# Sums of squares added up before TensorE, mLSTM gates on four column groups, and head scalings one step sooner

## The reference, cut to what matters

```python
def rms_norm(x, g):
    y = x * rsqrt(mean(x * x, axis=-1) + NORM_EPS)
    return y * g
...
def forgetting_attention(h, k, v, F, w_qg, q_gain, w_o):
    q = rms_norm(split_heads(q), q_gain)      # k likewise, in shared_kv
    s = einsum('bhqd,bhkd->bhqk', qb, k) * sm_scale + Fq - F
    p = softmax(where(kpos <= qpos, s, -inf))
    return einsum('bhqk,bhkd->bhqd', p, v)
...
def mlstm_inputs(...):
    # r: direction, h: head, e: 512 of the head, g: 8 = 4 input + 4 forget gates
    gates = (einsum('bhne,rheg->rbng', q, wq_g) + einsum('bhne,rheg->rbng', k, wk_g)
             + einsum('bhne,rheg->rbng', v, wv_g))
```

## Time and profile before

| | us |
|---|---|
| median of 3 runs (lowest, highest) | 2857.6 (2853.48, 2858.82) |
| profiled execution, its own time | 2853.31 |
| its span in the trace | 2851.5 |

### The profile page before, as it was taken

One profiled execution on the slowest core, in us unless ns is written; L12 is line 12 of the kernel. 1 busy time (PEld: TensorE's weight loads), 2 busy tenths in 40 slices (PEclk: granted clock), 3 DMA queues, 4 the chain that ended last, 5 costly groups with the idle time before them and its releaser, 6 DMA issues. The chain is left out here.

```text
span 2851.5 us, 36974 instructions
## 1 busy us (share of the span) xinstructions
PE 2675.0 (94%) x15206; PEld 2110.7 (74%) x15206; DVE 1320.5 (46%) x1833; ACT 756.1 (27%) x1408; POOL 1485.0 (52%) x474
## 2 busy tenths in 40 slices
PE   5899778999999999899999899999999999999998
PEld 4777777788887866678888786867676457878787
DVE  7747357665522315438454465415067855121211
ACT  4653321312201124423111123222223433011210
POOL 3653715677776752158777542422264027755574
PEclk9999979999999999999999899999999999999999
DMA  5222226465532221035555122222153226321221
GB/s 232 85 88 61 59 71 273 184 234 223 221 133 74 89 75 44 15 112 229 219 210 191 60 100 82 93 88 86 66 184 114 103 105 242 127 87 60 74 103 60
DMA packets 84048, 353.25 MB, mean 124 GB/s; under 512 B 26680, under 2 KB 38968, under 8 KB 46016
## 3 DMA queue, kind: packets, MB, share of 16 engines
q1 hardware_dynamic: 66048, 242.65, 23.3%
q10 hardware_dynamic: 17856, 108.54, 10.0%
HBM read 316.55 MB, written 34.60 MB: 123 GB/s over the span
## 5 line engine op out<-in xcount | busy, mean ns | idle before, releaser
L488 POOL TENSOR_TENSOR whi<-wraw,con_sb 128x2048 fp32r<-128x2048 f32 x170 | 615.5, 3620 | 1266.4 <-PE ps L544 1061.3
L490 POOL TENSOR_TENSOR wlo<-wraw,whi 128x2048 fp32r<-128x2048 f32 x170 | 802.2, 4719 | 13.3
L544 PE MATMUL ps<-hh,whi 128*128 128x512 f32 x952 | 372.6, 391 | 5.0 <-DVE hl L1760 5.0
L544 PE MATMUL ps<-hl,whi 128*128 128x512 f32 x952 | 370.9, 390 | 0.0
L544 PE MATMUL ps<-hh,wlo 128*128 128x512 f32 x952 | 370.9, 390 | 0.0
L544 PEld LDWEIGHTS ps<-hh,whi 128*128 128x128 f32 x952 | 179.1, 188 | 45.9 <-DVE hl L1760 5.4
L1976 DVE TENSOR_TENSOR midl<-rsq,midh 128x512 fp32r<-128x512 f32 x64 | 154.6, 2420 | 113.6 <-ACT midh L1934 113.6
L544 PEld LDWEIGHTS ps<-hh,wlo 128*128 128x128 f32 x952 | 179.0, 188 | 37.5
L544 PEld LDWEIGHTS ps<-hl,whi 128*128 128x128 f32 x952 | 179.2, 188 | 36.8
L544 PE MATMUL ps<-midh,whi 128*128 128x512 f32 x512 | 200.4, 391 | 0.0
L544 PE MATMUL ps<-midh,wlo 128*128 128x512 f32 x512 | 200.0, 391 | 0.0
(11 more groups left out here) (432 smaller groups left out, 5155.8 us busy)
## 6 DMA issues: line engine op xcount, KB each, us to landing
wraw<-wst SPq DMA_DIRECT2D x174, 1024.0 KB, 4.8
cond_w<-wcond ACTq DMA_DIRECT2D x68, 1024.0 KB, 4.8
first_w<-wcond SPq DMA_DIRECT2D x8, 1024.0 KB, 19.2
mod_w<-wcond SPq DMA_DIRECT2D x8, 1024.0 KB, 13.5
d_v<-ssb ACTq DMA_DIRECT2D x4, 1536.0 KB, 5.1
d_s<-ssb ACTq DMA_DIRECT2D x4, 1536.0 KB, 5.0
sld<-d_s SPq DMA_DIRECT2D x4, 1536.0 KB, 8.3
vld<-d_v SPq DMA_DIRECT2D x16, 384.0 KB, 3.3
```

The source lines that it names most:

```text
L488: pool.tensor_tensor(whi[:, s], wraw[:, f], C("zero").broadcast_to([P, BLK]), ALU.add).then_inc(sem("w_high"), 1)
L490: pool.tensor_tensor(wlo[:, s], wraw[:, f], whi[:, s].bitcast(F32), ALU.subtract).then_inc(w_split, 1)
L544: o = e.matmul(ps[:, b, :nt], w[:, k, mc], x[:, k0 + k, t0:t0 + nt], start=first and k == 0 and j == 0, stop=final and k == nk - 1 and j == 2)
```

## The change

Four edits. (1) The ring of four `sq` buffers becomes a total (`sq[:, 3]`, where square 0 is written) and a ring of three. DVE adds squares 1 to 6 to the total (`add_square`, behind each x tile's update); TensorE sums the total and square 7 alone, 4 matmuls each, both behind the last block. DVE waits for each square. (2) `squares_of_x` issues a one-element Sqrt (`sqrt_table`) ahead of the last Square. (3) The gates: the 16 columns are laid into a 32-column weight tile, the four feature tiles m of a source go to four groups of 32 output partitions, and `region` joins the four groups by a matmul with a 0/1 matrix (`C("gates")`, 64 KB more in the constants) ahead of the bias. (4) The attention: `scale(i+1, 0)` stands ahead of the turns at t = 1, and q and k are both scaled and normed at t = 1.

```diff
-                part = wif[d, t, c].reshape(4, P, 8).transpose(1, 0, 2)
-                gate[0, :, 4 * t:4 * t + 4, 64 * d:64 * d + 4] = part[:, :, :4]
-                gate[0, :, 4 * t:4 * t + 4, 64 * d + 32:64 * d + 36] = part[:, :, 4:]
+                gate[0, :, 4 * t:4 * t + 4, 8 * d:8 * d + 8] = wif[d, t, c].reshape(4, P, 8).transpose(1, 0, 2)
...
+    c["gates"] = np.zeros((P, P))
+    for j in range(4):
+        c["gates"][GW * j + np.arange(16), gate_row[0]] = 1.0
...
+        def sqrt_table(e):
+            e.activation(started[:, 0:1], C("zero"), ACT.Sqrt)
+
+        def squares_of_x(e, squared, added, beside=None):
             for k in range(KT):
+                if k == KT - 1:
+                    sqrt_table(e)
                 e.wait_ge(*AC.need(acc_free[k % NACC]))
+                if k >= 4:
+                    e.wait_ge(*added.at(k - 3))
+                    if beside is not None:
+                        e.wait_ge(*beside.at(k - 2))
+                e.activation(sq_ring[k % 3] if k else sq_total, x_sb[:, k], ACT.Square).then_inc(*squared.inc())
+        def add_square(e, k, squared, added):
+            if not 0 < k < KT - 1:
+                return
+            e.wait_ge(*squared.at(k + 1))
+            if k > 1:
+                e.wait_ge(*added.at(k - 1))
+            e.tensor_tensor(sq_total, sq_total, sq_ring[k % 3], ALU.add).then_inc(*added.inc())
...
             for j in range(4):
                 block(j)
-                for k in (2 * j - 2, 2 * j - 1):
-                    if k >= 0:
-                        square_sum(e, k, squared, summed)
-            square_sum(e, KT - 2, squared, summed)
-            square_sum(e, KT - 1, squared, summed)
+            e.wait_ge(*added.at(KT - 2))
+            sum_of(e, sq_total, 0, True, False)
+            e.wait_ge(*squared.at(KT))
+            sum_of(e, sq_ring[(KT - 1) % 3], 0, False, True).then_inc(*summed.inc())
...
+                    more = t == 1 and i + 1 < KT
+                    if more:
+                        scale(i + 1, 0)
                     turn(2 * s)
                     turn(2 * s + 1)
                     if t == 0 and i:
                         values(i - 1)
                         spread_sums(i - 1)
-                    elif t in (1, 2) and i + 1 < KT:
-                        scale(i + 1, t - 1)
+                    elif more:
+                        scale(i + 1, 1)
...
-                    elif t in (1, 2) and i + 1 < KT:
-                        norm(i + 1, t - 1)
+                    elif t == 1 and i + 1 < KT:
+                        norm(i + 1, 0)
+                        norm(i + 1, 1)
...
-                                o = pe.matmul(ps[:, b, :nt_], wg[:, 4 * j + m], src[:, m, t0:t0 + nt_],
-                                              start=j == 0 and m == 0, stop=j == 2 and m == 3)
+                                o = pe.matmul(ps[GW * m:GW * m + GW, b, :nt_], wg[:, 4 * j + m], src[:, m, t0:t0 + nt_],
+                                              start=j == 0, stop=j == 2)
...
+                for b, (t0, nt_) in zip((6, 7), spans):
+                    pe.matmul(ps[:, b, :nt_], C("gates"), gacc[:, t0:t0 + nt_], start=True, stop=True).then_inc(*gates_summed.inc())
...
-                step(dve.tensor_scalar(gz[:], gacc[:], V("bif", 0), None, ALU.add), sem("gz_ready"))
+                for b, (t0, nt_) in zip((6, 7), spans):
+                    dve.wait_ge(*gates_summed.at(b - 5))
+                    o = dve.tensor_scalar(gz[:, t0:t0 + nt_], ps[:, b, :nt_], V("bif", 0), None, ALU.add)
+                    o.then_inc(*VE.up(sem("gz_ready")))
```

More of the change, by code:

```diff
@@ L1667, in add_to_x, with add_to_x_once @@
             VE.loop(e, n // 4, four)
-        def add_to_x_once(e, gate):
+        def add_to_x_once(e, gate, squared, added):
             for m in range(KT):
@@ L1675, in add_to_x_once, with sum_of, summed_blocks @@
                                        ALU.add).then_inc(*VE.up(acc_free[b]))
-        def squares_of_x(e, squared, summed):
+                add_square(e, m, squared, added)
+        sq_total, sq_ring = sq[:, 3], [sq[:, j] for j in range(3)]
+        def sqrt_table(e):
+            e.activation(started[:, 0:1], C("zero"), ACT.Sqrt)
+        def squares_of_x(e, squared, added, beside=None):
             for k in range(KT):
+                if k == KT - 1:
+                    sqrt_table(e)
                 e.wait_ge(*AC.need(acc_free[k % NACC]))
-                square(e, k, x_sb[:, k], squared, summed)
-        def summed_blocks(e, block, squared, summed):
+                if k >= 4:
[10 more added lines that the diff above has]
+            e.tensor_tensor(sq_total, sq_total, sq_ring[k % 3], ALU.add).then_inc(*added.inc())
+        def sum_of(e, src, at, first, last):
+            for t in range(4):
+                o = e.matmul(ps[:, 7, at + t:at + t + 1], src[:, P * t:P * t + P], ones[:, 0:1], start=first and t == 0,
+                             stop=last, skip_group_check=True)
+            return o
+        def summed_blocks(e, block, squared, added, summed):
             for j in range(4):
                 block(j)
-                for k in (2 * j - 2, 2 * j - 1):
-                    if k >= 0:
-                        square_sum(e, k, squared, summed)
-            square_sum(e, KT - 2, squared, summed)
-            square_sum(e, KT - 1, squared, summed)
+            e.wait_ge(*added.at(KT - 2))
+            sum_of(e, sq_total, 0, True, False)
+            e.wait_ge(*squared.at(KT))
+            sum_of(e, sq_ring[(KT - 1) % 3], 0, False, True).then_inc(*summed.inc())
         phase_start()
@@ L1735, in _ @@
                     load_cond(act, n)
-                squares_of_x(act, squared, summed)
+                squares_of_x(act, squared, added)
             @block.vector
@@ L1773, in _ @@
                                              ALU.add).then_inc(*VE.up(acc_free[b]))
+                    add_square(dve, m, squared, added)
                     if m < 4:
@@ L1912, in last_block @@
                                     context_spread(pe)
-                            summed_blocks(pe, last_block, squared, summed)
+                            summed_blocks(pe, last_block, squared, added, summed)
                             if context:
                                 pe.wait_ge(*gained.at(KT))
-                                for t in range(4):
-                                    pe.matmul(ps[:, 7, 4 + t:5 + t], gained_sq[:, P * t:P * t + P], ones[:, 0:1], start=False,
-                                              stop=True, skip_group_check=True)
+                                sum_of(pe, gained_sq, 4, False, True)
                         else:
@@ L1954, in _ @@
                                 context_squares(act)
[L1955 to L1959, removed]
+                            squares_of_x(act, squared, added, beside=gained if context else None)
                             continue
@@ L2005, in _ @@
                                 down_tile(m)
[L2006 to L2009, removed]
+                                if context:
+                                    gained_square(m)
+                                    if m == 1:
+                                        dve.wait_ge(*gained.at(1))
+                                add_square(dve, m, squared, added)
                             cond_ends(dve)
@@ L2784, in two_tiles @@
                              final=k == 1, open_bank=open_bank)
-            summed_blocks(e, two_tiles, squared, summed)
+            summed_blocks(e, two_tiles, squared, added, summed)
         def region(d, s):
@@ L2922, in _ @@
                 linear(pe, "z", h2h, h2l, part=(2, 8), tokens=((TX, T),))
-                wide_out(pe, "mo", y_low, squared, summed)
+                wide_out(pe, "mo", y_low, squared, added, summed)
             @block.scalar
@@ L3259, in _ @@
                 linear(pe, "fz", hh, hl)
-                wide_out(pe, "fo2", y_low, squared, summed)
+                wide_out(pe, "fo2", y_low, squared, added, summed)
             @block.scalar
@@ L3370, in _ @@
                 VE.skip(acc_ready, 2 * ET)
-                add_to_x_once(dve, lambda m: ada1[:, 16 + m:17 + m])
+                add_to_x_once(dve, lambda m: ada1[:, 16 + m:17 + m], squared, added)
         res = tiles("res", 32, KT)
```

39 lines of the change are left out of this document (22 added, 17 removed).

## The result

| | changed kernel | before |
|---|---|---|
| median us (lowest, highest; runs) | 2791.14 (2788.58, 2792.69; 4) | 2856.25 (2853.48, 2858.82; 4) |
| profiled execution us, span | 2790.31, 2788.3 | 2853.31, 2851.5 |

The ratio is 0.9771, 95% interval 0.9754 to 0.9788: 65 us faster, where 74 were forecast against the median; between the two profiled executions 63.0 where the sum said 73.3. The time lies in the range and 9 us above the number.

The account below looks back on a forecast made before the run. TensorE, busy 94% of the span, was taken as the bound; 2853.3 - 33.3 (norms) - 43.9 (gates) + 3.6 (attention) + 0.3 (constants) = 2780.0 us, 2784.3 against the median; stated 2782, range 2772 to 2802.

Parts of the forecast that it names:

- Gates, 45.5 less 1.6: Gates on four column groups: 11.4 us saved per head, 45.5 for four, less 1.6 for joining at `region`.
- the attention's values on two groups: Attention's value matmuls, 64 columns wide: 4.3 us one after the other, took 2.37; basis for four gate groups overlapping.
- Rivals 1, 2 and 3: Gates: only two column groups overlap, 2797, chance 0.14; no overlap, 2827, 0.07; slower than before, 2892, 0.03.
- rival 4: More than forecast: attention gives 5.9 us or clock stays up at several ends, 2763 to 2772; chance 0.09.
- Rival 3: Gates: loads wait for the matmul ahead to drain, nothing overlaps, 32.4 us per head, 2892 in all; chance 0.03.
- Norm ends without a second DVE operation: Ends of layer 0's MLP, `mo`, `fo2`: 6.0 us saved each, `fo` 6.7; DVE's added additions cost nothing.
- MLP of layer 1, 5.3: Norm end of layer 1's MLP: 5.3 us saved, 1.7 at the end and the rest in the middle.
- outer bound of 3.8: Layer 1's MLP: if POOL gets in between two DVE operations, up to 3.8 of the 5.3 us go.
- `wo`, 3.3: Norm end of `wo`, where DVE is full: 1.8 us saved in the middle and 1.5 at the end.
- the range up to 2: `wo`: if POOL gets in between, up to 2 of the 3.3 us go; in the range only.
- Attention, +3.6: Attention: k scaling waits for q's norm, 0.5 us more per pair, seven pairs, 3.6 us lost.
- Clock, credited at nothing: Behind norm ends: a shorter chain may keep more clock, under 2 us at each of five ends, or cost nothing.

Follow-up runs that it names:

- e1: Changed kernel with squares 1 to 6 of each norm end written to a PSUM bank instead of SBUF; 2782.46 us, ratio to before 0.974.
- e2: Changed kernel with the attention's three edits undone, back to the order of before; 2789.53 us, ratio to before 0.976.
- e7: Changed kernel unchanged, timed again on one chip as neighbour of a timed variant; 2791.29 us, ratio to before 0.9774.
- e3: Changed kernel without the one-element Sqrt ahead of the last square, so the table loads behind the phase's end at five ends; single time 2802.63 us.
- e4: Changed kernel with the gates' loops turned round, three matmuls of one column group directly behind each other; single execution 2805.03 us.

## Why the prediction was right, and where it was off

- **Gates, 45.5 less 1.6: right.** Three heads gave 11.5 to 11.6 each (11.4 forecast), the fourth with the joining 10.4, of which 0.3 is lost again right behind it (9.8 forecast). The row that carried it was the attention's values on two groups, read as "two gave all of two". Rivals 1, 2 and 3 fell with it; rival 4 fell with the attention, which took time and gave none. (Rival 3 has each record going to another group; it is each matmul, whose two records stay on one group. Its price hardly depends on that.) At the 3.07 times that the Trainium skill ("TensorE: Matmul & The Clock Gate", "Measured speedup vs the span model") has for four row groups a head would have taken 5.1 us; it took 4.0, a factor of 3.9.
- **Norm ends without a second DVE operation: right.** 5.5, 6.5, 7.0 and 6.2 us for 6.0, 6.7, 6.0 and 6.0. The slow additions were there, 2.3 to 3.1 us, and hid as said.
- **MLP of layer 1, 5.3: mis-sized, gave 0.4.** The mechanism stood in the text (POOL getting in between two DVE operations), but as an outer bound of 3.8; the sum has nothing for it. It cost 4.9: 5.3 came back in e1. So the term that was mis-sized is that of the waits in this place, where two stand in a row and POOL starts a new operation between them. The earlier trace rows had the price of one such wait: 3.27 us, and in this place there are two per tile. The rest of the 4.9 over the bound is about 1 us of lower clock behind TensorE's wait, for which the forecast had no term.
- **`wo`, 3.3: mis-sized twice, gave 1.3.** Here the cover was gone from the start, 24 operations of 1.21 us, so three additions of 2.2 to 3.4 us moved the later x updates. The sum has nothing for this, the range up to 2; by e1 it cost 3.5. TensorE waited 2.7 us for the last addition. Without that wait, in e1, `wo` gives 4.8 in place of 3.3: the root comes 3.4 us sooner after the last block, and 1.5 was taken. The two errors hide a part of each other.
- **Attention, +3.6: right in mechanism, place and size.** +4.1 by the pairs (0.58 for 0.5 each).
- **Clock, credited at nothing: right on average.** Between the two profiled executions it cost the changed kernel 3.2 us around the end of the attention (1.7 in the last values, 1.5 in `fo`'s first matmuls). e2 and e7 show that the slow values are no part of the change; where the clock falls was not settled. A shorter chain kept more of the clock at one end at most: in the 12 us behind the root the granted clock is 0.72 in place of 0.60 at `mo`, but 0.60 in both kernels at layer 0's MLP, and 0.58 in place of 0.67 behind `wo`.

So of the 10 us that are missing between sum and profiled execution, 4.9 come from the waits for POOL in layer 1's MLP, 2.0 from `wo`, 3.2 from the clock at the attention's end, 1.0 from the later weights in the scan and 0.5 from the attention; `mo` and the gates with their joining gave 1.7 more than forecast, and 0.3 is spread over the rest. The range had room for the waits and for the attention (8 us together), but none of it was meant for the clock or the weights: in that the time still lies within it there is some luck.

## What to carry to other kernels

Work moved from TensorE to DVE is free only per place, not per kernel: ask at each place how many two-SBUF-input operations stand in a row beside POOL's long ones, since the second in a row can wait for a whole POOL operation again. Here one input in PSUM took that away entirely (36 additions, 0.693 us at most). Narrow matmuls that sit on different column groups should alternate between groups in program order: the same 24 took 4.0 us alternating and about 7.2 by group.

When an effect of 5 us is sought in a time that spreads over 9, compare stage borders of two traces, and time the pair on one chip before believing a single number; e3's time alone would have spoken for the wrong theory.

## What the hardware showed that I had not expected

- A DVE addition of two SBUF tiles took from 0.68 to 5.10 us in one program; with one operand in PSUM 0.681 to 0.693. POOL paid too: the `wlo` at 1579.64, which began 0.47 us before DVE's gain-weighted sum ended, took 4.95 us in place of 4.62. The Trainium skill ("SBUF — State Buffer", "SBUF: two separate sides") calls this an exclusive lock between a DVE operation with two SBUF inputs and a GpSimd operation that reads SBUF: the one that starts first has it for its whole length. The trace agrees on both sides, with 29 additions that ended 0.55 us behind POOL's operation, and with POOL's 0.33 us.
- Four column groups gave a factor of 3.9 in plain fp32. In e4 a matmul of the next group started at 1745.63, ahead of one of the group before that precedes it in the program and started at 1746.06.
- Two executions of one program differed by 1.7 us in one group of 16 records: 2.37 us at a granted clock of 1.00 (e7) and 4.07 at 0.58 (the changed kernel).
